# Two blocks on one core: gate rows by way of device memory, and modulation sums by transposes

## What is computed

```python
mod = silu(c) @ w_ada + b_ada                  # 2048 x 12288 weights, one for each block
sh1, sc1, gt1, sh2, sc2, gt2 = split(mod, 6)
h = rmsnorm(x) * (1 + sc1) + sh1
x = x + gt1 * (mixer(h) @ w_out)               # first gate: along the channels
h = rmsnorm(x) * (1 + sc2) + sh2
x = x + gt2 * ((silu(h @ w_gate) * (h @ w_up)) @ w_down)   # second gate
```

## Time and profile before

| | us |
|---|---|
| median of 3 runs | 2545.31 |
| lowest and highest | 2545.03, 2549.61 |
| the profiled execution | 2548.68 |
| its span, first to last instruction | 2547.0 |
| TensorE busy | 2471.6 (97%) |
| VectorE busy | 1789.0 (70%) |
| ScalarE busy | 1089.0 (43%) |

### The profile page before, as it was taken

The page is one execution under the profiler, slowest core; times in us unless marked ns, Lnnn a source line. Parts: engine busy times, 40 slices in busy tenths (PEclk is TensorE's granted clock), DMA queues, the critical chain, the costliest instruction groups (busy, mean ns, idle before and its releaser), DMA issues.

```text
span 2547.0 us, 31132 instructions
## 1 busy us (share of the span) xinstructions
PE 2471.6 (97%) x11854; PEld 2035.6 (80%) x11854; DVE 1789.0 (70%) x1779; ACT 1089.0 (43%) x1252; POOL 222.4 (9%) x397
## 2 busy tenths in 40 slices
PE   4899999999999999999999999999999999999999
PEld 3679458888888888879997778778888888888887
DVE  6878867888888888778775445666688555555565
ACT  2035115444444444464346556544544444444443
POOL 4412210111111111001110000000010000000000
PEclk8899999999999999999999999999999999999999
DMA  9999976898889888547985554355588555555554
GB/s 367 380 332 369 402 293 209 314 328 310 324 313 326 316 319 303 196 157 280 343 279 165 168 168 151 104 177 182 198 317 293 183 194 185 196 183 197 182 182 149
DMA packets 290560, 638.82 MB, mean 251 GB/s; under 512 B 21754, under 2 KB 34556, under 8 KB 290076
## 3 DMA queue, kind: packets, MB, share of 16 engines
q1 hardware_dynamic: 233808, 432.22, 50.0%
q0 software_dynamic: 56096, 205.02, 21.5%
q10 hardware_dynamic: 556, 0.18, 0.0%
HBM read 635.28 MB, written 2.10 MB: 250 GB/s over the span
## 4 chain that ended last, share of the span: by engine, by line
PE 89%; DVE 5%; ACT 3%; DMA 3%; issue 1%; POOL 0%; DVEq 0%; ACTq 0%; POOLq 0%
PE PS L1729 87%; DMA R<-in_w_ada 3%; DVE R L1045 2%; ACT WHI L551 1%; DVE WLO L1025 1%; PE PS L1964 1%; PE PS L1850 0%; PE PS L1881 0%; ACT R L629 0%; PE PS L1871 0%; ACT L915 0%; ACT L559 0%; ACT L907 0%; ACT L905 0%; ACT R L640 0%
## 5 line engine op out<-in xcount | busy, mean ns | idle before, releaser
L1025 DVE TENSOR_TENSOR WLO<-RAW,WHI 128x1024 fp32r<-128x1024 f32 x760 | 929.5, 1225 | 621.9 <-ACT WHI L551 620.2
L551 ACT ACTIVATE WHI<-RAW 128x1024 fp32r<-128x1024 f32 x760 | 804.8, 1061 | 1114.2 <-PE PS L1729 1100.3
L1729 PE MATMUL PS<-WHI,H 128*128 128x512 f32 x4064 | 1264.3, 392 | 11.2 <-DVE WLO L1025 7.8
L1729 PEld LDWEIGHTS PS<-WHI,H 128*128 128x128 f32 x4064 | 755.4, 188 | 178.5 <-DVE WLO L1025 19.0
L1729 PE MATMUL PS<-WLO,H 128*128 128x512 f32 x2032 | 792.3, 390 | 0.0
L1729 PEld LDWEIGHTS PS<-WLO,H 128*128 128x128 f32 x2032 | 381.8, 188 | 80.9
L1045 DVE SCALAR_TENSOR_TENSOR R<-R,CA 128x1024 f32<-128x1024 f32 x326 | 417.4, 1281 | 39.9 <-DMA R<-in_w_ada 32.0
L1729 PE MATMUL PS<-WHI,HID 128*128 128x512 f32 x1280 | 395.6, 390 | 0.0
L485 POOL DMA_DIRECT2D R<-in_w_ada x284 | 150.3, 529 | 1606.8 <-DVE R L1042 567.9
L1729 PEld LDWEIGHTS PS<-WHI,HID 128*128 128x128 f32 x1280 | 239.2, 188 | 48.9
L1729 PE MATMUL PS<-WLO,HID 128*128 128x512 f32 x640 | 249.3, 390 | 0.0
(11 more groups left out here) (227 smaller groups left out, 1299.7 us busy)
## 6 DMA issues: line engine op xcount, KB each, us to landing
R<-in_w_ada POOLq DMA_DIRECT2D x348, 512.0 KB, 6.7
RAW<-in_w_in SPq DMA_DIRECT2D x88, 1024.0 KB, 5.5
RAW<-in_w_ffn_in SPq DMA_DIRECT2D x88, 1024.0 KB, 5.0
RAW<-in_w_ffn_gate SPq DMA_DIRECT2D x44, 1024.0 KB, 5.9
RAW<-in_w_ffn_up SPq DMA_DIRECT2D x44, 1024.0 KB, 5.3
RAW<-in_w_ffn_down SPq DMA_DIRECT2D x44, 1024.0 KB, 8.6
RAW<-in_w_ffn_out SPq DMA_DIRECT2D x44, 1024.0 KB, 5.0
RAW<-in_w_out SPq DMA_DIRECT2D x32, 1024.0 KB, 6.5
```

The lines of the kernel that those rows point to most:

```text
L551: nc.scalar.activation(WHI[j][:, :, :], RAW[slot][:, 2 * half:2 * half + 2, :], ACT.Copy)\
L1025: nc.vector.tensor_tensor(WLO[j][:, :, :], RAW[slot][:, 2 * half:2 * half + 2, :], WHI[j][:, :, :].bitcast(F32), ALU.subtract).then_inc(lo ...
L1729: return nc.tensor.matmul(o, a, b, start=start, stop=stop, skip_group_check=True)
```

## The change

Two things. First, a gate row is now made so: TensorE transposes the 16 columns of the modulation that hold the gate to 16 x 128 (`row_turn`, one instruction), ScalarE copies this to a small tile ROW16, SyncE writes it to device memory (8 KB) and reads it back to all 128 partitions at once (a 1 MB read of one 8 KB row). Both transfers are in SyncE's own list between weight loads, each behind waits (for k = 2 the write stands behind W_in's two small loads for the rotary key, the read behind the loads of w_proj_mla, the last ones before W_out's). The diagonals, their matmuls and the four copies are gone; readers wait for the transfer. Second, groups 4 to 9 are summed as the later ones: transposes, then the reduce. The sum of group 6 moves from sub-step 8 to 9. For k = 2 the transpose moves from the second W_out to the second group of W_in of block 2.

```diff
-SUM_IN_W_OUT = {8: 6, 17: 7, 26: 8, 31: 9}
-ROW_IN_W_OUT = {10: 0, 11: 1, 12: 2, 13: 3}
+SUM_IN_W_OUT = {9: 6, 17: 7, 26: 8, 31: 9}
+ROW_TURN_IN_W_OUT = 6
+        ROW16 = place("ROW16", [KT, P])
+        row_dram = nc.dram_tensor("gate_rows", (4, D), F32, kind="Internal").ap()
...
+            def row_to_dram(k):
+                sp.wait_ge(row_ev, k + 1)
+                sp.dma_start(row_dram[k:k + 1, :].rearrange("o (r n) -> (o r) n", n=P), ROW16[:, :]).then_inc(row_out, 16)
+
+            def row_from_dram(k, freed, value):
+                sp.wait_ge(freed, value)
+                sp.wait_ge(row_out, 16 * (k + 1))
+                sp.dma_start(GT_ROW, row_dram[k:k + 1, :].to_broadcast([P, D])).then_inc(gt_row, 16)
...
-                with sp.Fori(2, NF - 1) as i:
+                with sp.Fori(2, NF - 2) as i:
...
+                gate_up(NF - 2)
+                row_to_dram(k)
+                for n in range(4):
+                    load(wd, (NF - 3) * 4, n * COLS)
+                    if n == 0:
+                        row_from_dram(k, x_step, 4 * k)
...
-            for g, q in W_OUT1:
+            for n, (g, q) in enumerate(W_OUT1):
                 load(w_out, 4 * q, g * COLS)
+                if n == 7:
+                    row_to_dram(0)
+                if n == 9:
+                    row_from_dram(0, yf_quad, 2)
...
+            row_to_dram(2)
...
+            row_from_dram(2, o_ev, 4)
...
-            def gate_row(k, n):
-                act.wait_ge(gt_mm, 4 * k + n + 1)
-                nc.scalar.activation(GT_ROW[:, n * 512:(n + 1) * 512], MISC, ACT.Copy).then_inc(gt_row, 1)
+            def gate_row(k):
+                if k:
+                    act.wait_ge(row_out, 16 * k)
+                act.wait_ge(row_mm, k + 1)
+                nc.scalar.activation(ROW16[:, :], MISC[0:KT, 0:P], ACT.Copy).then_inc(row_ev, 1)
...
-                if c.ada_group.at < 10:
-                    nc.vector.tensor_tensor(MOD[:, bass.ds(at, 8)], SMALL[:, 0:8], PRM[:, bass.ds(at, 8)], ALU.add)\
-                        .then_inc(ada_bias, 1)
-                else:
-                    step(nc.vector.tensor_reduce(SUM8, flat("D").rearrange("p (a b) -> p a b", a=8), AX_X, ALU.add))
...
+                step(nc.vector.tensor_reduce(SUM8, flat("D").rearrange("p (a b) -> p a b", a=8), AX_X, ALU.add))
...
-            def diagonals(k, gate, quads=range(4)):
-                if k:
-                    dve.wait_ge(gt_mm, 4 * k)
-                for t in (4 * q + i for q in quads for i in range(4)):
-                    ins = nc.vector.tensor_scalar(DIAG[:, t, :], ident, MOD[:, gate + t:gate + t + 1], None, ALU.mult)
...
-                dve.wait_ge(gt_row, 4 * k + n + 1)
+                dve.wait_ge(gt_row, 16 * (k + 1))
...
-            def ada_turn():
+            def ada_turn(acc=ACC):
...
-            def gate_row(k, n):
-                pe.wait_ge(diag_done, 4 * k + n + 1)
...
-                for t in range(4):
-                    ins = mm(MISC[:, t * P:(t + 1) * P], ones, DIAG[:, 4 * n + t, :], True, True)
-                ins.then_inc(gt_mm, 1)
+            def row_turn(k, gate, groups):
+                pe.wait_ge(ada_bias, groups)
+                if k == 2:
+                    pe.wait_ge(ft_in, 16)
+                nc.tensor.transpose(MISC[0:KT, 0:P], MOD[:, gate:gate + KT], ident).then_inc(row_mm, 1)
...
-                gate({3: hid_turn, 5: lambda: gate_row(k, 0)})
-                up(then={1: lambda: gate_row(k, 1), 5: lambda: gate_row(k, 2)})
+                gate({3: hid_turn, 5: lambda: row_turn(k, gate_at, c.ada_group.value())})
+                up()
...
-            group("B", then={2: lambda: gates(1), 4: lambda: gates(2), 5: lambda: ada_sum((ACC, G)[0]),
+            group("B", then={2: lambda: gates(1), 4: lambda: gates(2), 5: lambda: ada_turn((ACC, G)[0]),
...
                 if at in SUM_IN_W_OUT:
-                    ada_sum((ACC, G)[SUM_IN_W_OUT[at] % 2])
-                if at in ROW_IN_W_OUT:
-                    gate_row(0, ROW_IN_W_OUT[at])
+                    pe.wait_ge(row_ev, 1)
+                    ada_turn((ACC, G)[SUM_IN_W_OUT[at] % 2])
+                if at == ROW_TURN_IN_W_OUT:
+                    row_turn(0, mod_at(0, 2), 6)
...
-            group("B", kind="T")
+            group("B", kind="T", then={3: lambda: row_turn(2, mod_at(1, 2), 18)})
```

More of the change, by code:

```diff
@@ L706, in body @@
                             gate()
-                        if s in (8, 12, 16, 20) and rows:
-                            gate_row(k, (s - 8) // 4)
+                        if s == 8 and rows:
+                            gate_row(k)
                 body(skip=skip, subs=16, previous=False)
@@ L831, in _ @@
             nc.scalar.activation(tiles(8, 8), tiles(8, 8), ACT.Gelu_apprx_tanh).then_inc(gelu_done, 1)
-            for n in range(4):
-                gate_row(0, n)
+            gate_row(0)
             root_table(0)
@@ L1253, in win_body, with ffn @@
                         ada_beside(layer, s, 16)
-            def ffn(gate, k, a_free, c_free, groups, skip, layers):
+            def ffn(k, a_free, c_free, skip, layers):
                 def product(back=2):
@@ L1313, in body @@
                             add_down(2 + s // 2, 3)
-                        if s == 3 and rows:
-                            diagonals(k, gate)
                         if s == 6 and up:
@@ L1331, in ffn @@
                 c.leave(NF - 5)
-                dve.wait_ge(ada_bias, groups)
-                body(layer=layers[1], rows=True)
+                body(layer=layers[1])
                 for s in range(16):
@@ L1883, in turn, with w_out_groups @@
                 ins.then_inc(x_turned, 1)
-            def gate_row(k, n):
-                pe.wait_ge(diag_done, 4 * k + n + 1)
[L1888 to L1891, removed]
-                if k == 2:
-                    pe.wait_ge(h_quad, Q_WOUT2 + 4)
-                for t in range(4):
-                    ins = mm(MISC[:, t * P:(t + 1) * P], ones, DIAG[:, 4 * n + t, :], True, True)
-                ins.then_inc(gt_mm, 1)
-            def w_out_groups(k, quads, order=range(4), first={}):
-                rows = {6: 0, 7: 1, 8: 2, 9: 3}
+            def row_turn(k, gate, groups):
+                pe.wait_ge(ada_bias, groups)
+                if k == 2:
+                    pe.wait_ge(ft_in, 16)
+                nc.tensor.transpose(MISC[0:KT, 0:P], MOD[:, gate:gate + KT], ident).then_inc(row_mm, 1)
+            def w_out_groups(quads, order=range(4), first={}):
                 def after(at):
@@ L1956, in native_by_tokens, with ffn @@
                 c.all[pair].at += 1
-            def ffn(k, beside):
+            def ffn(k, beside, gate_at):
                 def hid_turn(more=1):
@@ L1999, in ffn @@
                 c.leave(NF - 5)
-                gate({3: hid_turn, 5: lambda: gate_row(k, 0)})
-                up(then={1: lambda: gate_row(k, 1), 5: lambda: gate_row(k, 2)})
-                rows_read = lambda: pe.wait_ge(gt_row, 4 * k + 4)
-                down(ada_after=0 if beside else None,
-                     then=lambda n: {0: {1: lambda: gate_row(k, 3)}, 1: {1: rows_read}}.get(n, {}))
+                gate({3: hid_turn, 5: lambda: row_turn(k, gate_at, c.ada_group.value())})
+                up()
+                row_read = lambda: pe.wait_ge(row_ev, k + 1)
+                down(ada_after=0 if beside else None, then=lambda n: {1: row_read} if n == 1 else {})
                 gate(previous)
@@ L2107, in _ @@
                     native(pair, src, q, q == 2, q == 1, "T", {s: lambda at=2 * n + s: w_out_after(at) for s in range(2)})
-            ffn(1, True)
+            ffn(1, True, mod_at(0, 5))
             group("A", kind="T", turned=(2, "DB"))
-            group("B", kind="T")
-            for _ in range(2):
-                group("A")
+            group("B", kind="T", then={3: lambda: row_turn(2, mod_at(1, 2), 18)})
+            for n in range(2):
+                group("A", then={7: lambda: pe.wait_ge(row_ev, 3)} if n == 0 else {})
                 group("B", ada_after=5)
```

47 lines of the change are left out of this document (18 added, 29 removed).

## The result

| | before | after |
|---|---|---|
| median (4 runs of each) | 2546.64 | 2530.44 |
| lowest, highest | 2545.03, 2549.61 | 2529.26, 2533.08 |
| the profiled execution | 2548.68 | 2530.02 |
| its span | 2547.0 | 2528.3 |

The ratio of after to before is 0.9934, with an interval of 0.9922 to 0.9947: 16.8 us faster, 13.5 to 19.9; the two medians of the table differ by 16.2. Predicted was 16.1, and 2529.2 for the time.

What follows compares the result with a forecast made beforehand. TensorE, busy 97% of the span, was taken as the bound. Terms -14.47 - 0.16 - 4.45 + 0.8 + 1.25 + 0.3 + 0.6 = -16.1 us from the median 2545.31 gave 2529.2; range 2525 to 2537 with the first two rivals.

Steps and rivals of the forecast that it cites:

- Gate rows removed: Both FFNs and both W_outs: four gates' pieces leave TensorE at about 3.62 us each, -14.47 us in all.
- Sums: First W_out: transposes replace products with ones, saving 0.89 us for each of groups 5 to 9, -4.45 us.
- transposes that do not overlap: Rival for the sums: eight transposes cost 2.2 us a group, total gain -9.5 us, time 2535.8; chance 0.04.
- One-instruction transposes: TensorE, one added per gate: 0.2 us each, between 0.11 and 0.87; +0.8 us for four.
- Group 9's uncovered reduce: Boundary behind the first W_out: VectorE's reduce has nothing to hide beside, +1.25 us with the semaphore step.
- Group 4's reduce: VectorE, ahead of the ada steps that release buffers for w_ada: 0 to 1.25 us, taken as +0.3.
- The stretch from 229.76 to the FFN: First W_out and boundary: one gate, five sums, one transpose and group 9's reduce, -6.62 us together.
- New wait in the second W_out: TensorE waits for a WLO at sub-step 10, while buffers are two: some 0.5 us, taken as +0.6, between 0 and 1.2.
- Queues: SP's added transfers: write lands within 12 us, read after 10.2 to 12, the added megabyte's 2.6 us hidden; cost 0.
- Loads set the first W_out: Rival: weight loads bound this stage, so it keeps its old time; total -9.8 us, 2535.5; chance 0.10.
- The other rivals: SP held by the row's write, 2550 and above, chance 0.03; an unnamed wait in the first 370 us, near 2541, chance 0.07.
- the named last moment: First W_out: load 10 must be issued by 319 - 12 = 307; each microsecond later costs one.

Runs made afterwards that it cites:

- The split residual: Changed kernel with the second W_out's first residual split, its addition moved behind the WLO of sub-step 10: 2531.23 against 2548.89 for before, ratio 0.9929.

## Why the prediction was right, point by point

- **Gate rows removed.** -14.47, of it -3.62 in each FFN, with +0.2 for the transpose: -3.42 predicted, -3.46 and -3.49 measured. Run alone, the rows gave -14.8 where -13.4 was expected, well within the interval. The distance of starts was the right measure; by the busy time of 1.05 per piece the sum would have been 16.8.
- **Sums.** Between native matmuls eight transposes take 0.88 us, as in the FFN; the step held. The figure weighed there, some 275 ns for a transpose of bf16 data (the Trainium skill, "TensorE: Matmul & The Clock Gate", Part 4: PE-mode transpose), would make 2.2 us for eight in a row, and no place with eight in a row shows it; the measurement decides. One record of these transposes does last 272 ns on average, but they overlap. The rival of transposes that do not overlap falls with it.
- **One-instruction transposes.** +0.2 each taken, 0.11 to 0.12 measured, the low bound. Over four gates 0.3 us too much.
- **Group 9's uncovered reduce.** Confirmed from both sides: with products by ones in its place the boundary came 0.46 earlier, with the sum put under matmuls 3.07.
- **Group 4's reduce.** +0.3 taken. It ran at 212.04, ahead of the arrival that decides, and the profile shows no cost; the stretch before 229 us even came out 1.9 us shorter. That can't be put down to the change. Group 5's transposes start anywhere from 239.96 to 244.93 in the nine profiles of kernels that are the same up to there (240.04 in after); the two profiles with group 4 summed by ones, before and the rows alone, lie inside, at 241.94 and 241.79. So a cost of 0.3 can't be seen here either, and the 1.9 us of the first stretch lie within this scatter.
- **The stretch from 229.76 to the FFN.** -3.62 - 4.45 + 0.2 + 1.25 = -6.62 predicted, -6.64 measured.
- **New wait in the second W_out.** 0.5 predicted at sub-step 10, 0.54 measured there; the stage -3.62 - 0.16 + 0.6 = -3.18 predicted, -3.08 measured. The split residual took the wait away. But with it gone the stage became 0.8 to 0.9 shorter. So the term of 0.6 was too small, within its bound of 1.2, and the rest of the stage gave 3.9 to 4.0 where 3.78 was counted: two small errors that cancel. No run shows where the second one comes from.
- **Queues.** The result was right, all hidden, but by much less than the prediction had it. The write landed after 13.7 us, over the bound of 12; the read after 17.7, where 10.2 to 12 was taken. The bounds came from transfers in a kernel without the added megabyte. In the two runs without it, those of the sums alone, the median weight load took 12.3 and 12.1 us. Hence the row arrived at 307.8 and not at 302 to 304; the prediction's times don't have the 1.9 us of the first stretch, so by them it is 309.7. VectorE waited for it, 3.43 us, less than the 5 us that would have been a sign of being wrong, and 5.72 us ahead of group 9's reduce were left. The prediction had counted the 14.81 us ahead of group 9 alone as cover; before, VectorE also waited for TensorE 3.80, 4.74 and 1.01 us earlier in this W_out. The FFN's first tile landed at 360.0, which with the same 1.9 us is the 362 forecast.
- **Loads set the first W_out.** Wrong for one megabyte, but by 0.35 us. The argument against this rival was 12.0 us per load with over 20 allowed; behind the read the loads took 18.7 to 20.9 with 20.4 to 21.3 allowed. That part of "all hidden" held by luck. With a second megabyte the rival is right: 3.2 us. I gave it 0.10, which was too little.
- **The other rivals.** SP was not held by the write. But the price given there was too low: with load 10 issued 1.2 us past the named last moment, 3.8 us were lost and not 1.2. Waits that I had not named did come, 0.7 us of TensorE's weight loads, and no delay of its matmuls shows for them.
- **The total.** Without the first stretch, the profiles differ by 6.64 + 3.46 + 3.49 + 3.08 less the 0.1 of the transpose, 16.6 us, of 16.1 predicted.

## What to carry to other kernels

Where the chain runs through TensorE, count a removed group by the distance of its neighbours' starts, and an added transfer by what its megabytes take at the rate the queues already run at: in a full stretch the first may be hidden and the second is paid in full. Look at the landing of each load behind the new transfer, and at when the tile is first used; the median over the stage hid that 8.6 us of room had become 0.35. A reduction that ends a stage belongs ahead of the stage's last matmuls; here the move was worth 3.9 us, more than the reduce itself. When an experiment needs a wait of its own, look for that wait in its profile before its time is read.

## What the runs showed of the hardware

- A write of 8 KB from a queue whose engines are at 1.03 of their share landed after 12.9 to 14.3 us in ten profiles. In each it took as long as the megabyte load issued 0.4 us ahead of it, within 0.1 us. In the first FFN the same write took 4.6 to 9.2 us, and the least in the whole kernel was 3.8. The Trainium skill ("DMA: Bandwidth & Descriptors", Queues, rings and completion order) says that each DMA engine takes the descriptors of a ring in order, though a later one may finish its write first. By that a small transfer stands behind the large ones ahead of it; the numbers agree with that.
- The read of one 8 KB row to 128 partitions landed after 16.9 to 18.0 us there, 3.3 us longer than the weight load issued 0.5 us ahead of it. In the first FFN it took 8.4 to 10.0.
- The last six weight loads of the first W_out landed 7.5 us apart on average, before as after, with the DMA engines at 1.03 of their share. TensorE takes such a unit in 6.88 us and the sums between. So a stage can show TensorE busy all the time and lose room with every unit.
- A transpose of 16 columns between matmuls of 512 moved the next one by 0.11 to 0.12 us, an eighth of eight full ones, although its own record lasts 0.27.
- In these traces a wait of TensorE costs more than the idle in its row: 0.54 us of idle cost 0.8 to 0.9 by the distance of starts, and six idles of 1.6 us in all came with 3.2.
